# Two transformer blocks on one core: attention outputs made step by step, decay rows copied by one wide product, half of x loaded behind the first weight slab

## The reference, cut to what matters

```
hn = rms_norm(x, norm_mix_g);  u = hn @ w_in             # the first norm and the first product
s = q @ k.T * scale + bias_mask;  p = softmax(s)          # mla, fox: 8 heads each; second block: band, 8 heads
out[q, h] = sum_k p[q, k] v[k, h]                         # "outputs"
# ssm_branch, per chunk, 16 heads:
seg = a_cum[i] - a_cum[j];  decay = exp(seg) below the diagonal
y_diag = (C B^T * decay) @ (x dt);  y = y_diag + y_off + x * D
```

## Time and profile before

| | us |
|---|---|
| runs shown | 2061.78, 2066.54, 2067.72 |
| median | 2066.54 |
| the profiled execution | 2065.07 |
| its span, first to last instruction | 2063.3 |
| mean granted clock of TensorE | 0.993 |

### The profile page before, as it was taken

One profiled execution on the slowest core, in us unless ns is written; L12 is line 12 of the kernel. 1 busy time (PEld: TensorE's weight loads), 2 busy tenths in 40 slices (PEclk: granted clock), 3 DMA queues, 4 the chain that ended last, 5 costly groups with the idle time before them and its releaser, 6 DMA issues.

```text
span 2063.3 us, 23852 instructions
## 1 busy us (share of the span) xinstructions
PE 2012.3 (98%) x9782; PEld 1655.2 (80%) x9782; DVE 1143.2 (55%) x1672; ACT 792.8 (38%) x1121; POOL 91.9 (4%) x104
## 2 busy tenths in 40 slices
PE   7999999999999999999999999999999999999995
PEld 6887788878888888888888687888888888888884
DVE  5757657577444765366378877743444443234245
ACT  5547543354423433133332535532233432133142
POOL 0004400110000000000010400000000000000000
PEclk9999999999999999999999999999999999999998
DMA  4320022212333332332343132232233232232231
GB/s 132 102 82 22 19 85 90 89 62 66 122 102 99 85 99 85 102 102 81 104 127 98 42 92 91 73 102 96 88 102 102 82 102 85 99 103 95 89 132 42
DMA packets 164443, 184.47 MB, mean 89 GB/s; under 512 B 6759, under 2 KB 125798, under 8 KB 164334
## 3 DMA queue, kind: packets, MB, share of 16 engines
q1 hardware_dynamic: 160718, 173.98, 26.6%
q10 hardware_dynamic: 2912, 6.83, 1.0%
q0 software_dynamic: 704, 2.13, 0.3%
HBM read 180.81 MB, written 2.12 MB: 89 GB/s over the span
## 4 chain that ended last, share of the span: by engine, by line
PE 73%; DVE 2%; issue 2%; ACT 1%; POOL 0%; POOLq 0%; DVEq 0%
PE ps L443 24%; PE ps L445 23%; PE ps L444 23%; PE ps L600 0%; ACT HH L1338 0%; DVE X L2686 0%; PE ps L573 0%; DVE arena L2684 0%; PE ps L586 0%; DVE X L2690 0%; ACT arena L1326 0%; DVE HL L1940 0%; DVE arena L1993 0%; PE ps L979 0%; PE ps L1013 0%
## 5 line engine op out<-in xcount | busy, mean ns | idle before, releaser
L443 PE MATMUL ps<-HH,WH 128*128 128x512 f32 (+1 forms) x1464 | 561.5, 384 | 7.7 <-DVE HL L1940 5.1
L1823 DVE TENSOR_TENSOR WL<-W,WH 128x2048 fp32r<-128x2048 f32 (+2 forms) x162 | 366.2, 2261 | 363.5 <-ACT WH L1288 355.5
L444 PE MATMUL ps<-HL,WH 128*128 128x512 f32 (+1 forms) x1464 | 557.6, 381 | 0.0
L445 PE MATMUL ps<-HH,WL 128*128 128x512 f32 (+1 forms) x1464 | 557.5, 381 | 0.0
L1288 ACT ACTIVATE WH<-W 128x2048 fp32r<-128x2048 f32 (+2 forms) x163 | 307.3, 1887 | 293.8 <-DMA W<-in_w_ff_dram 122.7
L443 PEld LDWEIGHTS ps<-HH,WH 128*128 128x128 f32 x1464 | 276.3, 189 | 63.2 <-issue 5.2
L445 PEld LDWEIGHTS ps<-HH,WL 128*128 128x128 f32 x1464 | 276.4, 189 | 52.9
L444 PEld LDWEIGHTS ps<-HL,WH 128*128 128x128 f32 x1464 | 276.4, 189 | 51.6 <-issue 0.2
L443 PE MATMUL ps<-WH,arena_r 128*128 128x512 f32 (+1 forms) x616 | 239.5, 389 | 1.6 <-issue 1.6
L444 PE MATMUL ps<-WL,arena_r 128*128 128x512 f32 (+1 forms) x616 | 239.2, 388 | 0.0
L445 PE MATMUL ps<-WH,arena_r 128*128 128x512 f32 (+1 forms) x616 | 239.1, 388 | 0.0
(11 more groups left out here) (355 smaller groups left out, 2248.0 us busy)
## 6 DMA issues: line engine op xcount, KB each, us to landing
W<-in_w_in_dram SPq DMA_DIRECT2D x50, 1024.0 KB, 5.2
W<-in_w_ff_dram SPq DMA_DIRECT2D x32, 1024.0 KB, 5.3
W<-in_ffn_w_up_dram SPq DMA_DIRECT2D x44, 512.0 KB, 5.1
W<-in_w_gate_dram SPq DMA_DIRECT2D x16, 1024.0 KB, 5.1
W<-in_ffn_w_down_dram SPq DMA_DIRECT2D x10, 1024.0 KB, 5.0
W<-in_w_out_dram SPq DMA_DIRECT2D x8, 1024.0 KB, 5.0
W<-in_w_branch_dram SPq DMA_DIRECT2D x8, 1024.0 KB, 5.0
W<-in_w_br_ssm_dram SPq DMA_DIRECT2D x4, 1024.0 KB, 5.3
```

The source lines that it names most:

```text
L443: pe.matmul(out_, st[0], mv[0], start=first, stop=False)
L444: pe.matmul(out_, st[0], mv[1], start=False, stop=False)
L445: return pe.matmul(out_, st[1], mv[0], start=False, stop=last)
L1823: dve.tensor_tensor(WL[:, j % RING, 0:n], W[:, j % RING, 0:n], plain(WH[:, j % RING, 0:n]), ALU.subtract).then_inc(slab_lo, 1)
```

## The change

Three edits. (1) `outputs(k-4)` is made in each step k, in both attention loops; DVE's, ACT's and POOL's loops are as they were. (2) `arow` is one matmul of 512 columns against a column of ones; the selection has moved to POOL, which writes 16 "diagonals" (selector times decay pieces, 48 x 512), alternately on partitions 0 to 47 and 64 to 111, and the decay pieces are copied to partitions 64 to 111 by DVE. (3) ACT loads x tiles 0 and 1, SP tiles 2 and 3 behind slab 0; ACT squares and DVE norms tiles 2 and 3 after the first half's eviction, and the band table follows them.

```diff
 # PE, attention
                     if step >= LAG:
                         turns(step - LAG)
-                    if step >= LAG + 2 and step % 2 == 1:
-                        outputs(step - LAG - 2)
+                    if step >= LAG + 1:
                         outputs(step - LAG - 1)
 # PE, scan
                     def arow(q):
+                        i = 4 * t + q
+                        rs = slice(64 * (i % 2), 64 * (i % 2) + 48)
                         b = bank(("ai", t, q))
-                        for j in range(4):
-                            h = 4 * q + j
-                            mm = pe.matmul(b[:, j * P:(j + 1) * P], bc(pick[0:48, h:h + 1], [48, P]),
-                                           decay_pieces[:, tok], start=True, stop=True)
-                        mm.then_inc(pe_done, 1)
+                        pe.wait_ge(diagonals_ready, i + 1)
+                        pe.matmul(b[:, :], bc(unit[rs, 0:1], [48, P]), split_at(19456, S)[rs, :],
+                                  start=True, stop=True).then_inc(pe_done, 1)
 # SP, after slab 0
+                    for t in range(2, NT):
+                        sp.dma_start(X[:, t, :], xr[:, t, :]).then_inc(x_in[t], 16)
 # POOL, scan
+                def diagonal(i):
+                    t, q = divmod(i, 4)
+                    rs = slice(64 * (i % 2), 64 * (i % 2) + 48)
+                    if i >= 2:
+                        use(pool, ("ai", (i - 2) // 4, (i - 2) % 4))
+                    pool.tensor_tensor(split_at(19456, 4, P)[rs], bc(plain(mask_r[rs, t * P:(t + 1) * P]).unsqueeze(1), [48, 4, P]),
+                                       bc(pick[rs, 4 * q:4 * q + 4].unsqueeze(2), [48, 4, P]), ALU.mult)\
+                        .then_inc(diagonals_ready, 1)
+                    pool.wait_ge(diagonals_ready, i + 1)
+                diagonal(0)
+                diagonal(1)
                 for t in range(NT):
...
                     pool.tensor_tensor(hv(x), hv(x), bc(drow[:, :].unsqueeze(2), HQ), ALU.mult).then_inc(xd_ready, 1)
+                    pool.wait_ge(xd_ready, t + 1)
+                    for i in range(4 * t + 2, min(4 * t + 6, 4 * NT)):
+                        diagonal(i)
 # ACT, start
-                    for t in range(NT):
+                    act.wait_ge(consts, 1)
+                    for t in range(2):
                         act.wait_ge(x_in[t], 16)
-                        act.wait_ge(consts, 1)
                         square(t, n)
                     for q in range(4):
                         split_piece(0, q)
                     taken(act, "gain")
                     evict(0)
+                    for t in range(2, NT):
+                        act.wait_ge(x_in[t], 16)
+                        square(t, n)
                     split(1)
 # DVE, start
-                    for t in range(NT):
-                        if t == 2:
-                            dve_rel_table()
-                        made(t)
+                    made(0)
+                    made(1)
...
                     lows(0)
+                    made(2)
+                    made(3)
+                    dve_rel_table()
                     split(1)
 # DVE, scan
-                dve.tensor_tensor(pick[0:48, :], ident[0:48, 0:SH], ident[0:48, 32:32 + SH], ALU.add)
-                link(dve.tensor_copy(decay_pieces, SS[0:48, :]))
-                dve.tensor_tensor(decay_pieces[32:48, :], SS[0:SH, :], plain(decay_pieces[0:SH, :]), ALU.subtract)
+                dve.tensor_copy(unit[:, :], ones[:, 0:1])
+                for r in (0, 64):
+                    dve.tensor_tensor(pick[r:r + 48, :], ident[r:r + 48, r:r + SH],
+                                      ident[r:r + 48, r + 32:r + 32 + SH], ALU.add)
+                link(dve.tensor_copy(mask_r[0:48, :], SS[0:48, :]))
+                link(dve.tensor_tensor(mask_r[32:48, :], SS[0:SH, :], plain(mask_r[0:SH, :]), ALU.subtract))
+                dve.tensor_copy(mask_r[64:112, :], plain(mask_r[0:48, :]))
```

More of the change, by code:

```diff
@@ L125, in build @@
         drow = sb("drow", [P, SH])
-        pick = sb("pick", [P, SH], F32R)
+        pick = sb("pick", [P, SH])
+        unit = sb("unit", [P, 1], F32R)
         ps = [ctx.enter_context(nc.psum_tensor(f"ps{i}", [P, 512], F32)) for i in range(NB)]
@@ L221, in build @@
         one_in = sem("one_in")
+        diagonals_ready = sem("diagonals_ready")
         gain_in = sem("gain_in")
@@ L745, in pe_ssm @@
                 SS, EB = at(19456, S), at(25088, NT, P)
-                decay_pieces = mask_r[0:48, :]
                 gemm_t_long("z", full, 2216, hnt, 0, between=after_heads[0])
@@ L1143, in _ @@
                 if i == 1:
+                    xr = A["x"][0].rearrange("(t p) d -> p t d", p=P)
+                    for t in range(2, NT):
+                        sp.dma_start(X[:, t, :], xr[:, t, :]).then_inc(x_in[t], 16)
                     for ap, start, n in first_params[1:]:
```

## The result

The changed kernel takes 2105.28 us (median of 4 runs, 2095.40 to 2107.83), the kernel before 2067.13 beside it: a ratio of 1.0182, with an interval of 1.0165 to 1.0198. It is 38 us slower, where I had forecast 11.4, and lies outside my range. Of its four runs the one of 2095.40 has a mean granted clock of 0.986, the other three, from 2105.02 on, 0.981 or 0.982. The profiled execution took 2107.83, its span 2105.9, at a mean granted clock of 0.981 (before 0.993).

The account below looks back on a forecast made before the run. PE, busy 98% of the span, was taken as the bound. Outputs +20, rows -5.6 and start -3.0 gave +11.4 on the profiled 2065.1, so 2076.5, or 2078 as the runs' median; range 2068 to 2087.

Parts of the forecast that it names:

- part 1: Attention loops, outputs in each step: PE waits for DVE's copy out of bank 7 and pairs lengthen, +20 us.
- the 1.9 of my bound: PE's standstill per pair before the copy of bank 7 ends, 1.9 us, used for the lower bound of 13.
- second leg: Part of an attention pair after scores(3), where DVE sets the pace with no gap; 4.89 us in a fox pair.
- DVE catches up: Rival, chance 0.12: in the attention loops the pair grows by half of what was walked, +10 - 8.6, 2068 us.
- The other side: Rival, chance 0.08: bank 7's wait does not pace the attention loop; DVE's copy falls before PE asks.
- The edits without effect on each other and part 1's groups alone: Rival, chance 0.05: only the attention loops' extra output groups cost, +7 - 8.6, 2065 us.
- third rival: Chance 0.12: the whole plus POOL's diagonals or the late DRAM send holding DVE or PE, 3 to 8 us more, 2084.
- Prices: PE times of scores, turns and outputs from the earlier trace, such as 1.39 for scores of t = 2.
- with no second pause of the clock: Condition of the start's best bound, a saving of 4.5 us.
- Part 2: Decay rows: `arow` as one 512-column matmul saves 0.35 us, 16 times, -5.6 us.
- the bound that I had written (-3.2): Decay rows' smallest saving, 0.2 us each if the weight load is not hidden.
- Part 3: Start: slab 0 lands sooner, PE's first product at 12.8 and restart at 22.0, -3.0 us.

Follow-up runs that it names:

- e4: Changed kernel with nine useless 128x512 products on PE ahead of each wait for bank 7; 2086.58 us, ratio 1.0104.
- e5: Changed kernel with DVE's copy out of bank 7 moved to the head of its iteration; 2074.45 us, ratio 1.0039.
- e6: Changed kernel with odd pairs' outputs in bank 6, leaving six banks for scores and turns; 2069.09 us, ratio 1.0014.
- e2: Kernel before with only the wide row copies (one-matmul `arow`, selection on POOL); 2067.53 us, ratio 1.0009.
- e9: e2 with each wide row product issued twice; 2065.70 us, ratio 1.0002.
- e3: Kernel before with only the changed start (half of x behind slab 0); 2059.86 us, ratio 0.9980.
- e12: e8 with seven useless products in the start, ahead of the first turn of the small parameters; 2058.19 us, ratio 0.9962.
- e8: Kernel before with the changed start and two output banks, outputs still made two steps at a time; 2058.77 us, ratio 0.9963.
- e1: Kernel before with only the outputs made in each step; 2104.35 us, ratio 1.0192.
- e10: e2 with POOL's `xw` of the next tile put ahead of the diagonals; 2066.81 us, ratio 1.0005.

## Why the prediction was wrong

The mechanism of part 1 was right in each of its steps. The outputs of t = 0 stand behind a wait for DVE's copy out of bank 7, eight times, of 2.2 us in the first loop and up to 2.7 in band, 17.9 in all (forecast 17 to 20); an undisturbed mla pair is 13.78 long (14.0). With the clock held, e4, the program costs +20.1 in all, and +20.7 from the first loop on (its span is 19.5 over that of before, and its first loop begins 1.2 earlier). The forecast for part 1 was +20; a standstill is 2.2 and not the 1.9 of my bound, and the undisturbed pairs came out within 0.25 of what I walked. e5 and e6, which take the wait away, bring back most of it. The second leg held no slack: the rival "DVE catches up" fell. "The other side" was to hold if the wait per pair was under 0.4 us, and fell with waits of 2.2. "The edits without effect on each other and part 1's groups alone" fell with the eight waits. No run shows its +7 for the groups; e6's trace has 0.31 a group in its place, 6.2 for twenty. The third rival, a second new wait at POOL's diagonals or the DRAM send, fell too: PE's waits in the scan name neither (the 0.7 for line 2368 is the nearest to it), and the send was issued at 19.09.

**The step that failed is the pricing of what comes behind a standstill.** "Prices" were those of the trace of before, all at a granted clock of 1.00, and I summed the new pair from them: the standstill plus the same work. I had the clock in mind only in the start (a bound "with no second pause of the clock"). In the changed kernel the granted clock falls to about a half for part of the loop (0.51 from 226.00 to 236.50), and the work right behind the standstills takes about twice as long there (scores of t = 2 2.73 for 1.39), which makes 17.19 of a fox pair that I had at 12.5. That is a term of +19 us which the sum did not have at all, as large as the standstills themselves. My sum was 26.8 short: 18.7 of it is this term, 5.6 the rows, and some 2.5 the start, which in this profiled run gained 0.4 by the first loop and not 3.0. The two levels show in one and the same product, of 128 x 512: it takes 0.23 at a granted clock of 1.00 (388 to 391 us of the kernel before) and 0.43 at 0.50 (33.90 to 34.33 in the changed kernel). I could have asked of every new wait whether the kernel before had one as long inside its attention loops; the longest there was 0.65. And its trace had the sign at the start: behind the wait of 3.19 the clock is 0.50 from 15.49 to 18.

**Part 2**, forecast -5.6, measured 0 (e2: +1.1 between the medians, interval of the ratio 0 to +3.9). Two reasons, one shown by a row, one by an experiment. The saving on PE is smaller: from its start to the next product `arow` went from 0.58 to 0.42, where I had 0.23 and the 0.12 behind it, so 0.15 to 0.18 each are saved, under 3 us in all; the bound that I had written (-3.2) was the nearer number. And PE doesn't pace that stretch (e9), so even this is given back in waits for the low parts of slabs. POOL's 16 operations took 1.04 in the median (one 1.96), as forecast, and nobody waited for them directly.

**Part 3**, forecast -3.0. Slab 0 was in ACT's hands at 9.44 (9.0), PE's first product started at 13.21 (12.8), the restart was at 23.27 (22.0), 1.7 earlier than before. From the trace that is -1.7 to -2.3; alone, e3's median is 6.6 lower, the ratio says -4, and its clusters say -2.6 and -2.7. All traces together say the same: the first attention loop begins between 156.8 and 159.9 in the five without edit 3 (mean 157.9) and between 153.5 and 156.9 in the nine with it (mean 155.1), 2.8 earlier. So this part was about right, and one pair of traces can show much less of it, or more. In the trace of the changed kernel nearly all of it is gone again by the first attention loop (-0.4). What lies between is in the main the clock: the window 30 to 35 us has 0.64 in the changed kernel and 1.00 before, which has its own dip later (0.85 between 60 and 70, the changed kernel 1.00).

```profile
30.00:35.00 5.00, 3.19 (x9) 2.52 (x10) 3.38 (x3) 4.38 (x5) 0.00 (x0) 0.64 0.42 121
```

```profile
30.00:35.00 5.00, 2.60 (x16) 2.01 (x16) 1.72 (x3) 4.27 (x6) 0.00 (x0) 1.00 0.37 119
```

In e12's and e8's profiles these dips sit elsewhere in the start. That this is what makes the two clusters of runs was not shown run by run.

## What to carry to other kernels

Moving an operation earlier in one engine's queue is a request to every engine that releases it: find the releaser's place in its own queue first, and if it can't move, give the operation a second buffer (e6) or move the release (e5). Price a new standstill of TensorE twice, once for itself and once for the clock behind it; filling it with useless products tells the two apart in one run, and was worth 19 us here. A saving in a stretch counts only if that engine paces it, and doubling the operation there shows this more cheaply than removing it.

## What the runs showed of the hardware

- Six standstills of 2.2 us, from one to the next 13.8 to 17.2 us, in an otherwise busy stream, took the mean granted clock to 0.91, 0.83 and then 0.74 in successive windows. The lengths of the matmuls show where: none is longer behind the first standstill (which ends at 179.77), behind the second some 3 us of work are (195.25 to 198.55), behind the third some 7, behind each of the last three about 10, and the clock is full again before the next. Waits of 0.6 at the same places (e5) left it at 1.00. The 0.93 of the first window lies ahead of all six: there the matmuls are longer behind the wait of 0.95 for line 2034, at 164.38. e5 has that wait and that dip as well (0.83 between 160 and 170), e4 and e6 have the wait and kept 1.00. Band, with its two waits, had one dip (0.91 between 1200 and 1220). In e1's trace, with the same standstills, the clock was 1.00 from 170 to 220 us and 0.85 and 0.67 in the next two windows. Why some waits bring the clock down and others of the same length do not stays open.
- An operation of DVE with two inputs, `arena` and `rows`, got longer beside one of POOL's. The same operation of line 2322 takes 0.69 in the kernel before (there line 2297), and 1.73 in the changed kernel, where POOL's `xw` now runs beside it. The rows are of before's DVE, then of after's DVE and POOL:

```profile
437.72 0.69 DVE L2297 TENSOR_TENSOR arena<-arena,rows 128x512 f32<-128x512 f32 x1 [0.75 <-issue]
```

```profile
473.12 1.73 DVE L2322 TENSOR_TENSOR arena<-arena,rows 128x512 f32<-128x512 f32 x1 [0.76 <-issue]
```

```profile
472.39 1.91 POOL L1245 TENSOR_TENSOR arena<-arena 128x1024 f32<-128x1024 f32 x1
```

  That is 1.0 us on one operation. It is the same place at which PE waits 0.7 for line 2368, and that wait is absent in e10, where `xw` runs earlier and the operation takes 0.69 again.
- Four groups of outputs in a fox pair in place of two cost 0.31 a group with all waits away (10.08 in e6, 9.46 before without its wait); a 48-row product in between 128-row ones costs 0.19 beyond its own 0.23 (0.42 for one in e2, 0.65 for two in e9).
